# Sums of activations made before the feed-forward loop's first block, and one subtraction for the three low parts of a set

## The chip, the cores and the metric

The kernel runs on one core of one Trainium2 chip. Its time is the device time of one execution in microseconds (us); the time of a version is the median of its runs. The engines are TensorE (PE: matmuls and, overlapped with them, the loads of their stationary operand), VectorE (DVE), ScalarE (ACT), GpSimd (POOL) and SyncE (SP), which issues the large loads.

## The reference

Two attention layers, a feed-forward network (FF1), a mixer layer, a second feed-forward network (FF2) and a gated projection, all in fp32 on 256 tokens of width 2048. The change lies in the feed-forward networks:

```python
def swiglu(x, w_gate, w_up, w_down):
    return (jax.nn.silu(x @ w_gate) * (x @ w_up)) @ w_down
...
    u = rmsnorm_2(h, ff1_pre_g[i])
    h = h + 0.5 * rmsnorm_2(swiglu(u, ff1_w_gate[i], ff1_w_up[i], ff1_w_down[i]), ff1_post_g[i])
```

`w_gate` and `w_up` are 2048 x 5632, `w_down` is 5632 x 2048.

## The kernel before

**Split operands.** Each fp32 operand is held as a high part, a rounded copy made by ScalarE (`w_hi`, `x_hi`), and a low part, the original minus the high part, made by VectorE (`w_lo`, `x_lo`). A product is three matmuls: high by high, high by low, low by high. So VectorE and ScalarE go over every weight that is loaded.

**Blocks.** The hidden width 5632 is worked in `FB` = 11 blocks of 512. Block 0's gate and up products are plain (8 units of weights, `u0` to `u0+7`). Then `first_block_of_hidden` does two things at once: it finishes block 0's hidden values, and makes the gate and up products of the next block; after it come the four down units of block 0 (`down`, `down_added` on VectorE, which adds each 2-bank result to `out2`). Nine further turns (`block_of_hidden`, eight of them in hardware loops or `whole_block(i + 1)`) do the same for the following blocks.

**Seven products instead of eight.** From `first_block_of_hidden` on, gate and up products of a 2 x 2 scheme (two chunks of the contraction, two tiles of tokens) share work through sums: sums of activations (`xs`, made once per network by `x_sums`) and, for each set, three sums of weights (`ff_ws`, made by `first_sum`, `second_sums`, `third_sum`). ScalarE makes the high parts of a set in two instructions (`first_sums_hi` for sums 0 and 1, `third_sum_hi` for sum 2), VectorE the low parts in `sums_lo`. There are 3 sets in `first_block_of_hidden` (p = 1, 2, 3) and 5 in each later block: p = 0 to 3, and a second set for p = 3 (`DOUBLE`), whose activation sums are `half_xs`, made once per network by `half_x_sums` (ten instructions of 128 x 128), with a high part on ScalarE and a low part by `half_x_sums_lo`. TensorE waits for `half_xs_ready` once, just before its loop over the later blocks:

```python
                first_block_of_hidden()
                pe.wait_ge(half_xs_ready, no + 1)
                with pe.Fori(0, FB - 3) as i:
                    block_of_hidden(i + 1)
```

**What sets the order.** Every engine has its own queue, in the order in which this code is written; semaphores tie the queues. The down unit j = 3 uses the PSUM bank that `down_added` of j = 1 reads, so TensorE waits there for VectorE's second addition. SyncE loads a slot of weights when TensorE has used its last content.

Of the kernel before, what the change touches and what calls it, by code (L numbers as in the profile page):

```python
# [7 lines left out]
F32 = mybir.dt.float32  # L8
F32R = mybir.dt.float32r
I32 = mybir.dt.int32  # L10
ACT = mybir.ActivationFunctionType
ALU = mybir.AluOpType
# [70 lines left out]
def build(nc, t):  # L83
# [87 lines left out]
    SUMMED, SUMMED_FIRST, SUMMED_LAST = [0, 1, 2, 3], [1, 2, 3], [0, 1, 2, 3]  # L171
# [31 lines left out]
    with ExitStack() as ctx:  # L203
# [17 lines left out]
        with ExitStack() as masks_space:  # L221
            half_xs_hi = masks_space.enter_context(nc.sbuf_tensor("half_xs_hi", [P, 4, P], F32R))
# [3 lines left out]
        with ExitStack() as masks_space:  # L226
            masks_space.enter_context(nc.sbuf_tensor("ahead_of_half_xs", [P, 4 * P], F32))
            half_xs = masks_space.enter_context(nc.sbuf_tensor("half_xs", [P, 4, P], F32))
# [93 lines left out]
        ff_ws, ff_ws_hi, ff_ws_lo = (ws, other_ws), (ws_hi, other_ws_hi), (ws_lo, other_ws_lo)  # L322
# [1470 lines left out]
        def _(act):  # L1793
# [533 lines left out]
            def feed_forward(b, no, hname):  # L2327
# [4 lines left out]
                def hidden_hi(i, dst=h_hi, bank=6):  # L2332
                    for s in range(2):
                        act.wait_ge(st_turned, i * 2 + (turned_before[hname] + s + 1))
                        nc.scalar.activation(dst[:, 0:UC, s * P:(s + 1) * P],
                                             ps[:, bank + s, :].rearrange("p (k n) -> p k n", k=UC),
                                             ACT.Copy).then_inc(st_hi, 1)
# [33 lines left out]
                def up_second_hi(u, p, i):  # L2371
                    if p == DOUBLE and not (isinstance(i, int) and i == 0):
                        act.wait_ge(ws_made, group(i, p, 1) * 4 + 3)
                    half_hi(u + 2 * p, p, 1, 1, i, plain_hi_ready)
# [44 lines left out]
                def first_block_of_hidden():  # L2419
                    u = u0 + 8  # L2420
                    for p in SUMMED_FIRST:
                        gate_second_hi(u, p, 0)
                        if p == SUMMED_FIRST[0]:
                            x_sums_hi()
                            hidden_hi(0)
                        up_second_hi(u, p, 0)
                        gate_first_hi(u, p, 0)
                        first_sums_hi(0, p)
                        third_sum_hi(0, p)
                        up_first_hi(u, p, 0)  # L2430
                    down_hi(u + 8, 0, 0)
                    first_product_copied(u, 0)
                    down_hi(u + 8, 1, 0)
                    down_hi(u + 8, 2, 0)
# [37 lines left out]
                def whole_block(i):  # L2472
                    if isinstance(i, int):
                        first_block_of_hidden()
                    else:
                        block_of_hidden(i)
                    u = i * 12 + (u0 + 8)
                    down_hi(u + 8, 3, i)
                    hidden_silu(i)
                    next_first_quarter(u + 12, i + 1)  # L2480
                    if isinstance(i, int):
                        act.wait_ge(half_xs_made, 6 * (no + 1))
                        nc.scalar.activation(half_xs_hi[:], half_xs[:], ACT.Copy).then_inc(half_xs_hi_ready, 1)

                whole_block(0)
                with act.Fori(0, FB - 3) as i:
# [153 lines left out]
        def _(dve):  # L2640
# [4 lines left out]
            V = nc.vector  # L2645
# [30 lines left out]
            def splits(u, j0, n):  # L2676
                for k in range(n):
                    split_lo(u + k, (j0 + k) % RAW)
# [737 lines left out]
            def feed_forward(b, no, hname):  # L3416
# [64 lines left out]
                def half_x_sums_lo():  # L3481

                    dve.wait_ge(half_xs_hi_ready, no + 1)
                    V.tensor_tensor(half_xs_lo[:], half_xs[:], half_xs_hi[:].bitcast(F32),  # L3484
                                    ALU.subtract).then_inc(half_xs_ready, 1)
# [22 lines left out]
                def first_sum(u, p, i, h=0):  # L3508

                    n, j = group(i, p, h), 2 * p % RAW  # L3510
                    landed(u + 2 * p, j, h, i)
                    landed(u + (2 * p + 1), j + 1, h, i)
                    since = sums_since(i, p, h)
                    if not isinstance(n, int) or n >= since:
                        dve.wait_ge(ws_used, n - (since - 1))
                    V.tensor_tensor(ff_ws[sums_place(i, p, h)][:, 0], raw_half(p, 1, h)[:, 0], raw_half(p, 0, h)[:, 0],
                                    ALU.subtract).then_inc(ws_made, 1)
# [14 lines left out]
                def sums_lo(p, i, h=0):  # L3532

                    n, place = group(i, p, h), sums_place(i, p, h)
                    dve.wait_ge(ws_made, n * 4 + 4)
                    for m, c in enumerate((slice(0, 2), slice(2, 3))):
                        dve.wait_ge(ws_hi_ready, n * 2 + (m + 1))
                        V.tensor_tensor(ff_ws_lo[place][:, c], ff_ws[place][:, c], ff_ws_hi[place][:, c].bitcast(F32),
                                        ALU.subtract).then_inc(ws_ready, 1)

                def half_lo(p, m, h):

# [22 lines left out]
                def up_second_lo(p, i):  # L3565

                    dve.wait_ge(plain_hi_ready, plain_of(i, p) * 2 + 2)
                    if p == DOUBLE and not (isinstance(i, int) and i == 0):
                        dve.wait_ge(ws_made, group(i, p, 1) * 4 + 3)
                    half_lo(p, 1, 1).then_inc(plain_ready, 1)  # L3570
# [38 lines left out]
                def first_product():  # L3609

                    splits(u0 + 8, 0, 1)
                    x_sums(0)
                    splits(u0 + 9, 1, 1)
                    x_sums(1)
                    dve.wait_ge(ff_silu, h0 + 1)
                    dve.wait_ge(parts_used, u0 + 8)
                    for tt in range(NT):
                        k = V.scalar_tensor_tensor(hid[:, tt], silu[:, tt], rstd[:, tt:tt + 1], ps[:, tt, :],
                                                   ALU.mult, ALU.mult)
                    k.then_inc(hid_ready, 1)  # L3620
                    x_sums(2)
# [5 lines left out]
                    V.tensor_tensor(o, o, ps[:, bank:bank + 2, :], ALU.add).then_inc(added, 1)  # L3627

                splits(u0 + 6, 2, 2)
                first_product()  # L3630
                dve.wait_ge(added, added_before(no))

                def first_block_of_hidden():
                    u = u0 + 8
                    for p in SUMMED_FIRST:
                        gate_second_lo(p, 0)
                        if p == SUMMED_FIRST[0]:
                            x_sums_lo((0,))
                            hidden_lo(0)
                            x_sums_lo((1, 2))  # L3640
                        if p < 3:
                            up_second_lo(p, 0)
                        first_sum(u, p, 0)
                        second_sums(p, 0)
                        third_sum(p, 0)
                        sums_lo(p, 0)
                        gate_first_lo(u, p, 0)
                        up_first_lo(u, p, 0)
                        if p == 3:
                            up_second_lo(p, 0)  # L3650
                    splits(u + 8, 0, 1)
                    first_rest(0)
                    other_rests(0)
                    gates_added(0)
                    splits(u + 9, 1, 1)
                    ups_added(u)
# [44 lines left out]
                def whole_block(i):  # L3701
                    if isinstance(i, int):
                        first_block_of_hidden()
                    else:
                        block_of_hidden(i)
                    u = i * 12 + (u0 + 8)
                    down_added(u + 8, i, 0)
                    splits(u + 10, 2, 2)
                    gate_second_lo(0, i + 1)
                    hidden_product(i)  # L3710
                    if isinstance(i, int):
                        half_x_sums()
                    first_sum(u + 12, 0, i + 1)
                    down_added(u + 8, i, 1)
                    second_sums(0, i + 1)
                    third_sum(0, i + 1)
                    gate_first_lo(u + 12, 0, i + 1)
                    down_added(u + 8, i, 2)
                    sums_lo(0, i + 1)
                    down_added(u + 8, i, 3)  # L3720
                    up_first_lo(u + 12, 0, i + 1)
                    up_second_lo(0, i + 1)
                    if isinstance(i, int):
                        half_x_sums_lo()
                    hidden_lo(i + 1, bank=0)

                whole_block(0)
# [297 lines left out]
```

## Time and profile before

| | |
|---|---|
| median of 3 runs | 2811.15 us (2808.17 to 2815.12) |
| the profiled execution | 2812.0 us |
| its span | 2810.2 us |
| PE busy | 2782.3 us (99%) |
| DVE busy | 2293.3 us (82%) |
| ACT busy | 1499.6 us (53%) |
| FF1's loop and its surroundings, 930 to 1600 us | PE 663.55, DVE 629.01, ACT 361.08 us busy of 670 |
| DMA, mean over the span | 189 GB/s |

A busy time is the union of an engine's instructions; in a row of the timeline the bracket is the time that the engine sat idle before the instruction, with what ended it. Consecutive instructions on one engine overlap at their ends, so a row's duration is a little longer than the distance to the next row. Where the span is longer than PE's busy time, TensorE stood still.

### The profile page before, as it was taken

The numbers are of one execution on the slowest core, as the hardware profiler recorded it, in microseconds if no ns is written. First come the engines' busy times: TensorE is split into PE (matmuls) and PEld (weight loads), VectorE is DVE, ScalarE is ACT, GpSimd is POOL, SyncE is SP. The second block draws the span as 40 slices with busy tenths as digits, with TensorE's granted clock in tenths as the row PEclk, the third lists the DMA queues.
The fourth block names the chain that finished last, engine by engine and source line by source line (L and its number), as shares of the span: only waits on it lengthen the run. The fifth ranks groups of instructions, "written<-read, shape, count | busy, mean of one in ns | idle before, by whom it ended". The sixth has DMA issues, their size and how long they took to land.

```text
span 2810.2 us, 36083 instructions
## 1 busy us (share of the span) xinstructions
PE 2782.3 (99%) x13100; PEld 2322.0 (83%) x13100; DVE 2293.3 (82%) x2684; ACT 1499.6 (53%) x1785; POOL 14.5 (1%) x20
## 2 busy tenths in 40 slices
PE   9999999999999999999999999999999999999998
PEld 8888888888898878888888888888878888888887
DVE  6869857855565889999999877686798999999985
ACT  6544545554545555555555555655554555555564
POOL 0000000000000000000000000000000000000000
PEclk9999999999999999999999999999999999999999
DMA  7546355555545566666666658543566666666654
GB/s 252 199 157 198 117 183 182 194 185 175 165 151 196 179 186 205 200 197 206 201 199 200 206 165 270 179 154 128 195 189 180 199 195 205 198 195 208 214 189 157
DMA packets 279468, 530.74 MB, mean 189 GB/s; under 512 B 12225, under 2 KB 35921, under 8 KB 278849
## 3 DMA queue, kind: packets, MB, share of 16 engines
q1 hardware_dynamic: 278320, 527.02, 59.0%
q0 software_dynamic: 752, 2.04, 0.2%
q8 instruction: 73, 1.20, 0.2%
q14 instruction: 35, 0.28, 0.0%
q10 hardware_dynamic: 288, 0.20, 0.0%
HBM read 527.12 MB, written 2.10 MB: 188 GB/s over the span
## 4 chain that ended last, share of the span: by engine, by line
PE 95%; DVE 3%; DMA 1%; issue 0%; ACT 0%; SPq 0%; DVEq 0%; ACTq 0%
PE ps L867 18%; PE ps L868 18%; PE ps L870 17%; PE ps L1425 9%; PE ps L1427 9%; PE ps L1426 9%; PE ps L878 2%; PE ps L954 1%; PE ps L953 1%; PE ps L952 1%; PE ps L897 1%; PE ps L898 1%; PE ps L902 1%; PE ps L1133 1%; PE ps L1419 1%; PE ps L1113 1%
## 5 line engine op out<-in xcount | busy, mean ns | idle before, releaser
L2664 DVE TENSOR_TENSOR w_lo<-raw,w_hi 128x2048 fp32r<-128x2048 f32 (+4 forms) x301 | 661.2, 2205 | 189.4 <-ACT w_hi L1818 188.3
L1818 ACT ACTIVATE w_hi<-raw 128x2048 fp32r<-128x2048 f32 (+4 forms) x301 | 554.7, 1847 | 287.6 <-DMA raw<-in_ff_w_down 132.9
L867 PE MATMUL ps<-w_hi,x_hi 128*128 128x512 f32 (+4 forms) x1760 | 679.0, 386 | 2.2 <-ACT z L1851 0.9
L868 PE MATMUL ps<-w_lo,x_hi 128*128 128x512 f32 (+4 forms) x1760 | 669.6, 380 | 0.0
L870 PE MATMUL ps<-w_hi,x_lo 128*128 128x512 f32 (+4 forms) x1536 | 582.7, 379 | 0.0
L2359 ACT ACTIVATE w_hi<-raw 128x1024 fp32r<-128x1024 f32 x312 | 321.3, 1049 | 133.0 <-DMA raw<-in_ff_w_up 99.6
L867 PEld LDWEIGHTS ps<-w_hi,x_hi 128*128 128x128 f32 x1760 | 330.7, 188 | 63.5 <-issue 2.5
L868 PEld LDWEIGHTS ps<-w_lo,x_hi 128*128 128x128 f32 x1760 | 330.9, 188 | 58.6
L3544 DVE TENSOR_TENSOR w_lo<-raw,w_hi 128x1024 fp32r<-128x1024 f32 x312 | 373.4, 1218 | 4.5 <-ACT w_hi L2359 2.9
L870 PEld LDWEIGHTS ps<-w_hi,x_lo 128*128 128x128 f32 x1536 | 288.4, 188 | 53.3
L1425 PE MATMUL ps<-w_hi,x_hi 128*128 128x512 f32 x672 | 265.1, 395 | 9.3 <-DVE half_xs_lo L3484 9.2
L1427 PE MATMUL ps<-w_hi,x_lo 128*128 128x512 f32 x672 | 262.8, 391 | 0.0
L1426 PE MATMUL ps<-w_lo,x_hi 128*128 128x512 f32 x672 | 262.7, 391 | 0.0
L867 PE MATMUL ps<-w_hi,h_hi 128*128 128x512 f32 x640 | 250.4, 391 | 3.6 <-DVE z L3627 3.6
L868 PE MATMUL ps<-w_lo,h_hi 128*128 128x512 f32 x640 | 249.7, 390 | 0.0
L870 PE MATMUL ps<-w_hi,h_lo 128*128 128x512 f32 x640 | 249.7, 390 | 0.0
L1425 PEld LDWEIGHTS ps<-w_hi,x_hi 128*128 128x128 f32 x672 | 126.9, 189 | 37.1 <-issue 10.1
L1427 PEld LDWEIGHTS ps<-w_hi,x_lo 128*128 128x128 f32 x672 | 126.8, 189 | 26.7
L1426 PEld LDWEIGHTS ps<-w_lo,x_hi 128*128 128x128 f32 x672 | 127.0, 189 | 25.6
L867 PEld LDWEIGHTS ps<-w_hi,h_hi 128*128 128x128 f32 x640 | 120.5, 188 | 30.4 <-DVE z L3627 4.4
L870 PEld LDWEIGHTS ps<-w_hi,h_lo 128*128 128x128 f32 x640 | 120.5, 188 | 25.3
L868 PEld LDWEIGHTS ps<-w_lo,h_hi 128*128 128x128 f32 x640 | 120.4, 188 | 24.9
(526 smaller groups left out, 3997.3 us busy)
## 6 DMA issues: line engine op xcount, KB each, us to landing
raw<-in_w_in SPq DMA_DIRECT2D x139, 1024.0 KB, 5.1
raw<-in_ff_w_gate SPq DMA_DIRECT2D x144, 512.0 KB, 3.7
raw<-in_ff_w_up SPq DMA_DIRECT2D x144, 512.0 KB, 3.7
raw<-in_ff_w_down SPq DMA_DIRECT2D x144, 512.0 KB, 4.6
raw<-in_w_out SPq DMA_DIRECT2D x45, 1024.0 KB, 5.1
raw<-in_ff_w_gate SPq DMA_DIRECT2D x16, 1024.0 KB, 5.1
raw<-in_ff_w_up SPq DMA_DIRECT2D x16, 1024.0 KB, 5.2
raw<-in_ff_w_down SPq DMA_DIRECT2D x16, 1024.0 KB, 5.2
```

Of the source, the lines that this page charges most:

```text
L867: nc.tensor.matmul(o, x[0][:, k0 + c, s], hi[:, c, 0:width], start=first and c == 0, stop=False)
L868: nc.tensor.matmul(o, x[0][:, k0 + c, s], lo[:, c, 0:width], start=False, stop=False)
L870: m = nc.tensor.matmul(o, x[1][:, k0 + c, s], hi[:, c, 0:width], start=False, stop=last and c == n - 1)
L878: m = nc.tensor.matmul(ps[:, bank + tt, 0:width], x[1][:, k0 + c, tt * P:(tt + 1) * P], hi[:, c, 0:width], start=False, stop=last and c == ...
L897: nc.tensor.matmul(o, x[0][:, k0 + c, s], hi[:, c, 0:width], start=first and c == 0, stop=False)
L1425: nc.tensor.matmul(ps[:, bank, :], x[0], w[0], start=start, stop=False)
L1426: nc.tensor.matmul(ps[:, bank, :], x[0], w[1], start=False, stop=False)
L1427: return nc.tensor.matmul(ps[:, bank, :], x[1], w[0], start=False, stop=stop)
L1818: nc.scalar.activation(landed_part(w_hi, u, j), landed_part(raw, u, j), ACT.Copy).then_inc(hi_ready, 1)
L2359: nc.scalar.activation(w_hi[:, j, c], raw[:, j, c], ACT.Copy).then_inc(ready, 1)
L2664: V.tensor_tensor(landed_part(w_lo, u, j), landed_part(raw, u, j), landed_part(w_hi, u, j).bitcast(F32), ALU.subtract).then_inc(parts_read ...
L3544: return V.tensor_tensor(w_lo[:, j, c], raw[:, j, c], w_hi[:, j, c].bitcast(F32), ALU.subtract)
```

## The change

Three of its edits are one move. `half_x_sums()` goes from the end of block 0's work on VectorE (behind `hidden_product`) to the place behind units `u0+6` and `u0+7`, ahead of `first_product()`. `half_x_sums_lo()` goes from the end of `whole_block(0)` to p = 2 of `first_block_of_hidden`; the ScalarE instruction between the two goes from behind `next_first_quarter` to p = 2 too. The other edit is in `sums_lo`: one subtraction over all three sums, after the second of the two high parts, in the place of one over sums 0 and 1 and one over sum 2.

```diff
@@ ScalarE, first_block_of_hidden
                         if p == SUMMED_FIRST[0]:
                             x_sums_hi()
                             hidden_hi(0)
+                        if p == SUMMED_FIRST[1]:
+                            act.wait_ge(half_xs_made, 6 * (no + 1))
+                            nc.scalar.activation(half_xs_hi[:], half_xs[:], ACT.Copy).then_inc(half_xs_hi_ready, 1)
                         up_second_hi(u, p, 0)
@@ ScalarE, whole_block
                     next_first_quarter(u + 12, i + 1)
-                    if isinstance(i, int):
-                        act.wait_ge(half_xs_made, 6 * (no + 1))
-                        nc.scalar.activation(half_xs_hi[:], half_xs[:], ACT.Copy).then_inc(half_xs_hi_ready, 1)
@@ VectorE, sums_lo
                     dve.wait_ge(ws_made, n * 4 + 4)
-                    for m, c in enumerate((slice(0, 2), slice(2, 3))):
-                        dve.wait_ge(ws_hi_ready, n * 2 + (m + 1))
-                        V.tensor_tensor(ff_ws_lo[place][:, c], ff_ws[place][:, c], ff_ws_hi[place][:, c].bitcast(F32),
-                                        ALU.subtract).then_inc(ws_ready, 1)
+                    dve.wait_ge(ws_hi_ready, n * 2 + 2)
+                    V.tensor_tensor(ff_ws_lo[place][:], ff_ws[place], ff_ws_hi[place][:].bitcast(F32),
+                                    ALU.subtract).then_inc(ws_ready, 2)
@@ VectorE, ahead of the first product
                 splits(u0 + 6, 2, 2)
+                half_x_sums()
                 first_product()
@@ VectorE, first_block_of_hidden
                         if p < 3:
                             up_second_lo(p, 0)
+                        if p == SUMMED_FIRST[1]:
+                            half_x_sums_lo()
                         first_sum(u, p, 0)
@@ VectorE, whole_block
                     hidden_product(i)
-                    if isinstance(i, int):
-                        half_x_sums()
                     first_sum(u + 12, 0, i + 1)
...
                     up_second_lo(0, i + 1)
-                    if isinstance(i, int):
-                        half_x_sums_lo()
                     hidden_lo(i + 1, bank=0)
```

TensorE's queue is the same in both. First place: VectorE at the end of block 0's work in FF1, from `hidden_product` (L3605) on; L3470 to L3479 are `half_x_sums`, L3516 is `first_sum` of the next block's first set, L3627 is `down_added`, L3538 is `sums_lo`, L3544 the low half of a weight unit, L3484 `half_x_sums_lo`. Before:

```order
L3605 SCALAR_TENSOR_TENSOR z<-z,st 128x512 x2
L3470 TENSOR_TENSOR half_xs<-x_hi 128x128
...
L3479 TENSOR_TENSOR half_xs<-half_xs,x_lo 128x128
L3516 TENSOR_TENSOR z<-raw 128x512
L3627 TENSOR_TENSOR z<-z,ps 128x2x512
...
L3538 TENSOR_TENSOR ws_lo<-z,ws_hi 128x1024
L3538 TENSOR_TENSOR ws_lo<-z,ws_hi 128x512
L3627 TENSOR_TENSOR z<-z,ps 128x2x512
L3544 TENSOR_TENSOR w_lo<-raw,w_hi 128x1024 x2
L3484 TENSOR_TENSOR half_xs_lo<-half_xs,half_xs_hi 128x512
L3424 TENSOR_TENSOR h_lo<-ps,h_hi 128x4x128 x2
```

The same place in the changed kernel, where the lines behind `sums_lo` have a number one lower:

```order
L3604 SCALAR_TENSOR_TENSOR z<-z,st 128x512 x2
L3516 TENSOR_TENSOR z<-raw 128x512
L3626 TENSOR_TENSOR z<-z,ps 128x2x512
...
L3537 TENSOR_TENSOR ws_lo<-z,ws_hi 128x1536
L3626 TENSOR_TENSOR z<-z,ps 128x2x512
L3543 TENSOR_TENSOR w_lo<-raw,w_hi 128x1024 x2
L3424 TENSOR_TENSOR h_lo<-ps,h_hi 128x4x128 x2
```

Ten instructions between `hidden_product` and `first_sum` are gone from here, and so is the low part ahead of `h_lo`.

Second place: VectorE of the changed kernel where they went, between the low parts of unit `u0+7` and of `u0+8` (L2664), ahead of `x_sums` (L3439 and on):

```order
L2664 TENSOR_TENSOR w_lo<-raw,w_hi 128x2048 x2
L3470 TENSOR_TENSOR half_xs<-x_hi 128x128
...
L3479 TENSOR_TENSOR half_xs<-half_xs,x_lo 128x128
L2664 TENSOR_TENSOR w_lo<-raw,w_hi 128x2048
L3439 TENSOR_TENSOR xs<-x_hi 128x4x128
```

Before, the same rows read `x3` and then L3439 at once. Third place: VectorE of the changed kernel at p = 1 and p = 2 of `first_block_of_hidden`, with the merged subtraction (L3537) and `half_x_sums_lo` (L3484) behind four halves of weight units:

```order
L3530 TENSOR_TENSOR z<-raw,z 128x512
L3537 TENSOR_TENSOR ws_lo<-z,ws_hi 128x1536
L3543 TENSOR_TENSOR w_lo<-raw,w_hi 128x1024 x4
L3484 TENSOR_TENSOR half_xs_lo<-half_xs,half_xs_hi 128x512
L3516 TENSOR_TENSOR z<-raw 128x512
```

Here the merged instruction stands right behind `third_sum` (L3530), whose high part it now waits for; in the later blocks one or two halves of weight units stand between the two, or the first sums of the next set.

## Rows read from the trace of the kernel before

**Rows 1.** The page: TensorE's and VectorE's busy time.
```profile
PE 2782.3 (99%) x13100; PEld 2322.0 (83%) x13100; DVE 2293.3 (82%) x2684; ACT 1499.6 (53%) x1785; POOL 14.5 (1%) x20
```

**Rows 2.** TensorE's waits: total us, times, longest.
```profile
PE ps L1425 <- DVE half_xs_lo L3484: 9.2, 2, 4.7
PE ps L867 <- DVE z L3627: 3.6, 2, 1.8
```

**Rows 3.** Timeline of TensorE, FF1, block 0's down units and the loop's start.
```profile
1005.27 0.39 PE L867 MATMUL ps<-w_hi,h_hi 128*128 128x512 f32 x1
...
1023.54 0.50 PE L867 MATMUL ps<-w_hi,h_hi 128*128 128x512 f32 x1 [1.79 <-DVE z L3627]
...
1033.93 0.79 PE L1425 MATMUL ps<-w_hi,x_hi 128*128 128x512 f32 x1 [4.66 <-DVE half_xs_lo L3484]
...
1040.43 0.39 PE L1425 MATMUL ps<-ws_hi,xs_first 128*128 128x512 f32 x1
```

**Rows 4.** The same two points of TensorE, and VectorE's `first_sum`, one block later.
```profile
1076.47 0.39 PE L867 MATMUL ps<-w_hi,h_hi 128*128 128x512 f32 x1
...
1090.11 0.68 DVE L3516 TENSOR_TENSOR z<-raw 128x512 f32<-128x512 f32 x1
...
1103.20 0.39 PE L1425 MATMUL ps<-ws_hi,xs_first 128*128 128x512 f32 x1
```

**Rows 5.** The same two points of TensorE in FF2's block 0.
```profile
2079.89 0.39 PE L867 MATMUL ps<-w_hi,h_hi 128*128 128x512 f32 x1
...
2117.71 0.39 PE L1425 MATMUL ps<-ws_hi,xs_first 128*128 128x512 f32 x1
```

**Rows 6.** Stretches: length, each engine's busy time (instructions), granted clock, DMA.
```profile
2096.00:2117.00 21.00, 14.64 (x49) 11.39 (x48) 14.36 (x18) 7.82 (x10) 0.00 (x0) 0.76 0.40 116
...
1020.00:1029.00 9.00, 7.21 (x32) 5.55 (x30) 8.76 (x15) 6.74 (x8) 0.00 (x0) 1.00 0.54 150
```

**Rows 7.** Timeline of VectorE at the end of block 0, FF1.
```profile
1018.91 0.28 DVE L3470 TENSOR_TENSOR half_xs<-x_hi 128x128 f32<-128x128 f32 x1
...
1021.67 0.69 DVE L3516 TENSOR_TENSOR z<-raw 128x512 f32<-128x512 f32 x1
1022.28 1.21 DVE L3627 TENSOR_TENSOR z<-z,ps 128x1024 f32<-128x1024 f32 x1
...
1032.81 0.68 DVE L3484 TENSOR_TENSOR half_xs_lo<-half_xs,half_xs_hi 128x512 fp32r<-128x512 f32 x1
```

**Rows 8.** Groups of VectorE from 951.8 to 961.5 (FF1), 2026.8 to 2036.2 (FF2).
```profile
L2664 DVE TENSOR_TENSOR w_lo<-raw,w_hi 128x2048 fp32r<-128x2048 f32 x2 | 4.6, 2292 | 2.9 <-ACT w_hi L1818 2.9
L2664 DVE TENSOR_TENSOR w_lo<-raw,w_hi 128x2048 fp32r<-128x2048 f32 x2 | 4.6, 2292 | 2.6 <-ACT w_hi L1818 2.6
```

**Rows 9.** Timeline at p = 2 and p = 3 of block 0, FF1: ScalarE, VectorE.
```profile
979.93 1.06 ACT L2359 ACTIVATE w_hi<-raw 128x1024 fp32r<-128x1024 f32 x1 [1.56 <-DMA raw<-in_ff_w_up]
989.90 1.22 DVE L3544 TENSOR_TENSOR w_lo<-raw,w_hi 128x1024 fp32r<-128x1024 f32 x1 [0.70 <-ACT w_hi L2359]
992.65 0.69 DVE L3516 TENSOR_TENSOR z<-raw 128x512 f32<-128x512 f32 x1 [1.52 <-PE ps L1427]
```

**Rows 10.** Timeline of the third set, FF1: ScalarE, VectorE, TensorE's weight load.
```profile
995.30 0.63 ACT L2389 ACTIVATE ws_hi<-z 128x512 fp32r<-128x512 f32 x1
995.44 1.83 DVE L3538 TENSOR_TENSOR ws_lo<-z,ws_hi 128x1024 fp32r<-128x1024 f32 x2 [0.17 <-ACT ws_hi L2384]
997.56 0.19 PEld L1425 LDWEIGHTS ps<-ws_hi,xs_fourth 128*128 128x128 f32 x1
```

**Rows 11.** VectorE's groups by form, whole span: count, busy us, mean ns.
```profile
L3538 DVE TENSOR_TENSOR ws_lo<-z,ws_hi 128x1024 fp32r<-128x1024 f32 x60 | 73.1, 1218 | 0.5 <-ACT ws_hi L2384 0.3
L3538 DVE TENSOR_TENSOR ws_lo<-z,ws_hi 128x512 fp32r<-128x512 f32 x60 | 41.0, 683 | 0.0
```

**Rows 12.** The loop's tightest set: VectorE's subtractions, TensorE's weight load.
```profile
2393.61 1.82 DVE L3538 TENSOR_TENSOR other_ws_lo<-z,other_ws_hi 128x1024 fp32r<-128x1024 f32 x2
2395.82 0.19 PEld L1425 LDWEIGHTS ps<-other_ws_hi,xs_fourth 128*128 128x128 f32 x1
```

## Prediction

> **What bounds the kernel now.** I read the busy shares first. TensorE is busy 2782.3 us of a span of 2810.2 [rows 1], so it bounds the kernel and 27.9 us of standstill are all that an edit of other engines can win directly. TensorE's waits come next: who kept it? Two lines stand out, and both belong to the two feed-forward networks, once in each: 9.2 us for `half_xs_lo` and 3.6 us for `down_added` (L3627), together 12.8 us of the 27.9 [rows 2]. No wait for `ws_lo` or for any low part inside the loop is among them: the eighteen later blocks run without a gap on TensorE. So the change can gain only at block 0 of FF1 and FF2, and whatever it saves in the loop on VectorE is slack.
>
> Then the timeline at that place. After the long wait, TensorE does not take up its pace: in FF1 the first matmul takes 0.79 us where the ones further on take 0.39 [rows 3]. In FF2 the granted clock is 0.76 over the 21 us from the first wait on, so nearly half of them ran at 1.2 GHz instead of 2.4 [rows 6]. So a wait costs more than its length. I therefore don't add up waits, but measure the whole detour between two fixed points of TensorE's program: the first down matmul of block 0 and the first matmul on sums of weights of the next block. In FF1 that takes 1040.43 - 1005.27 = 35.16 us [rows 3]; one block later, with the same instructions and no wait, 1103.20 - 1076.47 = 26.73 us [rows 4]. The detour is 8.43 us. In FF2 it is 2117.71 - 2079.89 - 26.73 = 11.09 us [rows 5]. Together 19.52 us: 12.8 of waits and 6.7 of slow clock.
>
> **The move, what it removes.** Behind `hidden_product` ten small instructions take 1021.67 - 1018.91 = 2.76 us of VectorE [rows 7]. The second `down_added` stands behind them: it started at 1022.28 and will start at 1019.52, to end 1.21 us later at 1020.73. TensorE wants it when it has done three down units: its wait of 1.79 us ended at 1023.54, so it was done at 1021.75, less 0.16 for the overlap of two matmuls at the end, 1021.6 [rows 3]. 0.86 us to spare, so this wait goes altogether. The second wait is for `half_xs_ready`, whose low part ended at 1032.81 + 0.68 = 1033.49 [rows 7]; it is now made some 50 us earlier. What is late next there? With both gone TensorE comes to the loop at 1005.27 + 4 x 5.44 = 1027.0 (a down unit takes a third of 1021.6 - 1005.27). What it needs then are the third `down_added` and the low half of a weight unit. VectorE's remaining queue, shifted by 2.76 us or to the end of the TensorE unit that it adds, is then what it is in the later blocks: there L3516 starts 1090.11 - 1076.47 = 13.64 us behind the first down matmul [rows 4], here it will be 1018.91 - 1005.27 = 13.64 too, and those blocks have no wait. I take the whole detour, 19.52 us, as gained. From both sides: at least the 12.8 us of waits if the clock should drop anyway, at most 19.52.
>
> **The move, what it adds.** Nothing is added, three pieces stand elsewhere. The ten instructions (2.76 us) go ahead of unit `u0+8`'s low part. VectorE stood idle there, before that one and the next unit, for 2.9 us in FF1 and 2.6 in FF2, each time for ScalarE and the loads behind it [rows 8]. The 2.76 fill that; 0.2 us may stick out in FF2, with more idle time behind. Without this cover it would be 2.76 us of VectorE, some 15 us ahead of TensorE's need. The ScalarE piece (0.61 us) goes ahead of the instruction at 979.93, which waited 1.56 us for a load anyway [rows 9]. The low part (0.68 us, 0.61 to the next instruction) goes to p = 2; what it delays there is counted with the next edit. SyncE's and GpSimd's queues are not passed: cost 0.
>
> **One subtraction instead of two.** The form 128x1536 is not in the trace. 128x1024 takes 1218 ns, 128x512 takes 683, so 512 elements cost 535 ns and 128x1536 should take 1.75 us [rows 11]; half way from 1218 to the 2292 ns of 128x2048 [rows 8] is 1.76. It saves about 0.08 us of VectorE's queue in each of the 96 sets (the two took 1.83 together [rows 10]), 8 us in all, and none of it where TensorE waits: worth 0. What it costs is that sums 0 and 1 are ready later. In the loop the high part of sum 2 is done before VectorE comes to the subtraction, since other work stands between, so the delay is 1.75 - 1.22 = 0.53 us. The tightest of the 90 sets there: start 2393.61, end 2395.36 where the first ended at 2394.83; TensorE's first weight load comes at 2395.82 [rows 12]. 0.46 us to spare: cost 0.
>
> In block 0 the merged one stands right behind `third_sum` and has to wait for ScalarE's 0.63 us. Sets 1 and 2 push VectorE back by 0.6 us each, and the moved low part by 0.6 more: 1.8 us, before p = 3, against idle times of 0.70 and 1.52 us on the way [rows 9]. Absorbed. Set 3 is left: ScalarE's high part ends at 995.93, the merged one runs from about 996.0 to 997.75, and TensorE's weight load that needs it came at 997.56 [rows 10]. With a handover of 0.05 us (VectorE's L3627 ended at 1023.49 and TensorE started at 1023.54 [rows 3, 7]) TensorE stands for 0.25 us. Bounds: 0, if the handovers are shorter, and 0.5, if each takes longer. Twice, so 0.5 us lost.
>
> **The sum.** 19.5 gained, 0.5 lost: 19.0 us off the profiled execution's own 2812.0, which is 2793.0 us. That execution was 0.85 us above the median of the runs shown, 2811.15. Since the slow clock behind the waits differs from network to network (2.0 us in FF1, 4.7 in FF2) it will differ from run to run as well, and with it goes part of the 7 us spread of before. The time after has none of it, so I keep 2793 and take nothing off for the median. A change of under 0.3% (8.4 us) is about what a measurement of this kernel can't tell from none.
>
> **Rivals.** *Part of it stays.* If `first_sum` of the next block must wait for its load (in later blocks such waits occur), the second `down_added` comes later, and past 0.86 us TensorE waits again; or the loop's first block, entered 8 us sooner, has one short wait for a load. Against it: the same order works without a wait in the later blocks. Price: up to the 3.6 us of L3627 and up to one slow stretch of clock in each network (2.0 us by FF1): 2793 + 3.6 + 4.0 = 2800.6, middle 2798. Chance 0.13.
>
> *Short waits bring the slow clock.* The new wait of 0.25 us is small, but it could cost more than itself. For it: the waits for L3627 were 1.8 us long in both networks, and after FF2's the stretch shows 0.76; against it: after FF1's, of equal length, the granted clock is 1.00 [rows 6], and the new one is a seventh as long. Price 2 x 2.0 to 2 x 4.7 us: 2797 to 2802. Chance 0.05. The Trainium skill has such a rule ("TensorE: Matmul & The Clock Gate", section "A second HAM failure mode: psum-queue depth-cycling"): short idle times between groups of matmuls, if there are many, make the clock swing between its levels. By that rule the merged subtraction would be dear; that FF1's wait of 1.79 us left the clock at 1.00 speaks against it here.
>
> *Nothing moves.* The waits return elsewhere, because VectorE or the loads, not their order, limit block 0: TensorE would wait in the loop's first block for what it now reaches late. For it: VectorE is busy 8.76 of the 9 us from 1020 on [rows 6]. Against it: later blocks hold the pace of 26.73 us with the same work [rows 4]. Time within 0.3%, 2803 to 2811. Chance 0.06.
>
> *Slower.* The merged subtraction makes TensorE wait in the loop: one place, p = 3, five sets a block, 18 blocks. It has 0.46 us to spare at its tightest [rows 12]. To end 8.4 us above before it must cost 19.5 + 8.4 = 28 us, 1.5 us a block, so the sums would have to be ready 2 us later than worked out, with 1.75 us an instruction of more than 3.5. No row is near that: 2820. Chance 0.02.
>
> **How the numbers follow.** The forecast, 2793, has 0.74, with its own range from 2789 (no new wait, a somewhat faster execution) to 2797. The first two rivals reach to 2802. I put the range at 2788 to 2801.5; outside it are the last two rivals, 0.08, and some 0.08 of the others. Faster by over 0.3% (below 2802.7) are the forecast and the first two rivals, less a little for the unforeseen: 0.90. Same 0.07, slower 0.03.
>
> **What would show it.** Right: no row of TensorE waiting for `half_xs_lo` or for `down_added`; between the two fixed points 26.7 us in both networks; granted clock 1.00 from block 0's down units on; a wait of 0.2 to 0.3 us for `ws_lo` ahead of `xs_fourth`, once in each; VectorE's busy time 6 to 14 us lower; the form 128x1536 at 1.75 us. Wrong: a wait of TensorE for `ws_lo` inside the loop, or for a load in its first block; a slow clock behind the short wait in block 0.

## The result, and the profile after

The changed kernel takes 2792.03 us (median of 4 runs, 2791.79 to 2792.41), the kernel before beside it 2811.97 us (4 runs, 2808.17 to 2815.12): a ratio of 0.993, interval 0.9913 to 0.9947. The forecast was 2793.0 us. Its profiled execution took 2791.79 us, 20.2 less than that of before. The four runs scatter over 0.6 us where those of before scattered over 7. Of the runs told below, two of one kernel (3473 and 10009 us) stand far outside all others, for a reason that no trace shows, and are left out.

The page's first rows, the span and the busy times, beside [rows 1]:

```profile
span 2790.0 us, 35987 instructions
...
PE 2775.6 (99%) x13100; PEld 2318.9 (83%) x13100; DVE 2286.9 (82%) x2588; ACT 1499.7 (54%) x1785; POOL 14.5 (1%) x20
```

TensorE does the same 13100 matmuls in 6.7 us less busy time: that is not work saved, but clock. While TensorE works, the trace of before has it at half in four places, this one in one, in the mixer. VectorE has 96 instructions fewer and is busy 6.4 us less. TensorE's waits, the longest first, beside [rows 2]:

```profile
PE ps L897 <- ACT x_hi L2023: 1.7, 1, 1.7
PE ps L1304 <- POOL ones L818: 1.0, 1, 1.0
PE ps L867 <- ACT z L1851: 0.8, 1, 0.8
```

Both lines of [rows 2] are gone; what leads now lies outside the feed-forward networks. The two fixed points of TensorE, in FF1 and then in FF2, beside [rows 3] and [rows 5]:

```profile
1005.36 0.39 PE L867 MATMUL ps<-w_hi,h_hi 128*128 128x512 f32 x1
...
1027.12 0.39 PE L1425 MATMUL ps<-w_hi,x_hi 128*128 128x512 f32 x1
...
1032.12 0.39 PE L1425 MATMUL ps<-ws_hi,xs_first 128*128 128x512 f32 x1
...
2071.75 0.39 PE L867 MATMUL ps<-w_hi,h_hi 128*128 128x512 f32 x1
...
2098.52 0.39 PE L1425 MATMUL ps<-ws_hi,xs_first 128*128 128x512 f32 x1
```

26.76 and 26.77 us, where [rows 4] had 26.73: block 0 now runs like a later block. TensorE comes to the loop at 1027.12. The same stretches by engine (length; busy us of PE, PEld, DVE, ACT, POOL; granted clock; DMA), beside [rows 6]:

```profile
1005.00:1033.00 28.00, 28.00 (x129) 23.25 (x128) 26.77 (x26) 14.71 (x15) 0.00 (x0) 1.00 0.73 218
2071.00:2099.00 28.00, 28.00 (x130) 23.23 (x129) 26.78 (x25) 14.71 (x15) 0.00 (x0) 1.00 0.74 224
```

The clock is 1.00 in both. The one new cost is at the third set of block 0, beside [rows 10]: ScalarE's high part of sum 2, VectorE's merged subtraction, TensorE's weight load and matmul.

```profile
995.16 0.62 ACT L2389 ACTIVATE ws_hi<-z 128x512 fp32r<-128x512 f32 x1
...
995.91 1.76 DVE L3537 TENSOR_TENSOR ws_lo<-z,ws_hi 128x1536 fp32r<-128x1536 f32 x1 [0.90 <-ACT ws_hi L2389]
...
997.72 0.19 PEld L1425 LDWEIGHTS ps<-ws_hi,xs_fourth 128*128 128x128 f32 x1 [0.45 <-DVE ws_lo L3537]
...
997.30 0.39 PE L1427 MATMUL ps<-w_hi,x_lo 128*128 128x512 f32 x1
997.72 0.50 PE L1425 MATMUL ps<-ws_hi,xs_fourth 128*128 128x512 f32 x1
998.05 0.40 PE L1426 MATMUL ps<-ws_lo,xs_fourth 128*128 128x512 f32 x1
```

VectorE stood 0.90 us for the high part. The matmuls start 0.42 and 0.33 us apart in the place of 0.227 each, so TensorE lost 0.30 us. In FF2 they start 0.32 and 0.33 us apart, 0.20 us lost. The list of waits has neither: they fell into the overlap of two matmuls' ends, and show in the distances and in the weight load's bracket. The weight load in FF2:

```profile
2064.12 0.19 PEld L1425 LDWEIGHTS ps<-ws_hi,xs_fourth 128*128 128x128 f32 x1 [0.35 <-DVE ws_lo L3537]
```

The merged form and the moved sums, from VectorE's groups and timeline, beside [rows 11] and [rows 8]:

```profile
L3537 DVE TENSOR_TENSOR ws_lo<-z,ws_hi 128x1536 fp32r<-128x1536 f32 x60 | 105.2, 1754 | 4.9 <-ACT ws_hi L2389 4.9
...
951.40 0.29 DVE L3470 TENSOR_TENSOR half_xs<-x_hi 128x128 f32<-128x128 f32 x1
...
954.16 2.29 DVE L2664 TENSOR_TENSOR w_lo<-raw,w_hi 128x2048 fp32r<-128x2048 f32 x1
...
959.03 2.29 DVE L2664 TENSOR_TENSOR w_lo<-raw,w_hi 128x2048 fp32r<-128x2048 f32 x1
```

The ten instructions take 2.76 us again, and the low part of the unit behind them follows without idle time.

### The profile page after: what moved, and what is told of

It is laid out like the page before. It is cut to its first block, busy times and chain, and to the rows that moved or that the text cites. A ratio compares the mean times of both kernels' runs of the same rounds, so it can differ in the third digit from the quotient of the medians.

```text
span 2790.0 us, 35987 instructions
## 1 busy us (share of the span) xinstructions
PE 2775.6 (99%) x13100; PEld 2318.9 (83%) x13100; DVE 2286.9 (82%) x2588; ACT 1499.7 (54%) x1785; POOL 14.5 (1%) x20
## 4 chain that ended last, share of the span: by engine, by line
PE 98%; DVE 1%; DMA 0%; ACT 0%; issue 0%; SPq 0%; DVEq 0%; ACTq 0%
PE ps L867 19%; PE ps L868 19%; PE ps L870 17%; PE ps L1425 9%; PE ps L1427 9%; PE ps L1426 9%; PE ps L878 2%; PE ps L954 1%; PE ps L953 1%; PE ps L952 1%; PE ps L897 1%; PE ps L898 1%; PE ps L902 1%; PE ps L1133 1%; PE ps L1419 1%; PE ps L1113 1%
## 5 line engine op out<-in xcount | busy, mean ns | idle before, releaser
L2664 DVE TENSOR_TENSOR w_lo<-raw,w_hi 128x2048 fp32r<-128x2048 f32 (+4 forms) x301 | 661.5, 2207 | 183.9 <-ACT w_hi L1818 183.0
```

What stands on the lines that cost most here:

```text
L2664: V.tensor_tensor(landed_part(w_lo, u, j), landed_part(raw, u, j), landed_part(w_hi, u, j).bitcast(F32), ALU.subtract).then_inc(parts_read ...
```

## The experiments

All were timed beside the kernel before, four kernels to a chip. The edits are to the changed kernel unless said otherwise.

**The move alone.** `sums_lo` as before the change (two subtractions).

> The sums of activations are moved as in the change, the low parts of a set stay two instructions. Theory (the order at block 0's end is what the change gains, the merged subtraction costs its wait ahead of the third set): 0.6 us under the changed kernel's 2792.0, so 2791.4, no short wait at the third set (0.30 us in each network there), the stretch between the two fixed points 26.7 us. Rival 1 (the merged subtraction gives part of the gain, since VectorE is slower by 0.08 us a set without it): above 2793. Rival 2 (the two effects need each other): above 2797, with a wait for down_added back.

Measured: 2790.55 us (5 runs, 2790.05 to 2792.22), ratio 0.9926 (0.9914 to 0.9939). It has the whole gain. The changed kernel on the same chip had 2790.72, so the merged subtraction gives no part of it, and the 0.6 us that the moved sums alone were expected to be ahead can't be told in the medians (0.2 us apart); the spans of the profiled executions are 2788.8 and 2788.9 us. In its trace the matmuls at the third set start 0.23 us apart: the short wait is gone.

**The merged subtraction alone**, in the kernel before:

```diff
-                    for m, c in enumerate((slice(0, 2), slice(2, 3))):
-                        dve.wait_ge(ws_hi_ready, n * 2 + (m + 1))
...
+                    dve.wait_ge(ws_hi_ready, n * 2 + 2)
+                    V.tensor_tensor(ff_ws_lo[place][:], ff_ws[place], ff_ws_hi[place][:].bitcast(F32),
+                                    ALU.subtract).then_inc(ws_ready, 2)
```

> The kernel before with the merged subtraction alone. Theory: no gain, both waits stay (3.6 us for down_added, about 9.1 for half_xs_lo), one short wait of 0.3 us more in each network: within 2 us of the kernel before, so 2810 to 2814. VectorE's busy time about 6.5 us lower all the same. Rival (the merge gives part of the 20 us): 2808 or less.

Measured: 2811.5 us (11 runs, 2809.90 to 2813.61), the kernel before 2811.45 (17 runs); ratio 1.0 (0.9991 to 1.0009). Its page's busy times and its TensorE's waits:

```profile
PE 2780.7 (99%) x13100; PEld 2321.3 (83%) x13100; DVE 2287.2 (81%) x2588; ACT 1500.1 (53%) x1785; POOL 14.5 (1%) x20
...
PE ps L1425 <- DVE half_xs_lo L3484: 9.2, 2, 4.6
PE ps L867 <- DVE z L3626: 3.6, 2, 1.8
```

VectorE is busy 6.1 us less than in [rows 1], the two waits are the same to a tenth, and so is the time: nearly all of the work was saved where nobody waits for VectorE.

**Two subtractions in block 0, one in the later blocks**, run on two chips.

```diff
+                    if isinstance(i, int) and i == 0:
+                        for m, c in enumerate((slice(0, 2), slice(2, 3))):
...
+                        return
```

> The changed kernel with two instructions for the low parts in the three sets of block 0 and one in the later blocks. Theory: the 0.3 us wait ahead of the third set goes in both networks, 2791.4, the same as the move alone, as what the merged one saves in the loop is slack. Rival (the saving in the loop counts, because TensorE is kept now and then for a few tenths by VectorE there): 0.5 us or more under the move alone, 2790.9 or less.

> The changed kernel with two instructions for the low parts in block 0 and one in the later blocks, once more beside the changed kernel. Theory: 0.5 to 0.7 us under it by the trace (the two short waits ahead of the third sets), which is less than the runs scatter.

Measured: 2791.94 us over the four other runs of the first chip (2790.40 to 2792.94), and 2791.24 (5 runs, 2790.38 to 2792.57) on the second, where the changed kernel had 2791.54. The short wait is gone from the trace: TensorE's matmuls at the third set, first of this kernel on the second chip, then of the changed kernel there:

```profile
997.32 0.39 PE L1427 MATMUL ps<-w_hi,x_lo 128*128 128x512 f32 x1
997.54 0.39 PE L1425 MATMUL ps<-ws_hi,xs_fourth 128*128 128x512 f32 x1
```

```profile
997.71 0.39 PE L1427 MATMUL ps<-w_hi,x_lo 128*128 128x512 f32 x1
998.36 0.50 PE L1425 MATMUL ps<-ws_hi,xs_fourth 128*128 128x512 f32 x1 [0.27 <-DVE ws_lo L3537]
```

Here the changed kernel lost 0.53 us at this set in FF1, more than the 0.30 of its first profile. Spans: 2788.3 against 2788.9 us on the first chip, 2788.2 against 2789.8 on the second. Its profiled executions are the shortest of all, but that it is the best version isn't shown: beside the changed kernel its median is 1.2 us above on the first chip and 0.3 us below on the second, and the runs scatter by 2 us. The rival, 2790.9 or less, did not come; the saving in the loop is not told from nothing.

**The changed kernel again**, as the measure for the tenths of the others.

> The changed kernel once more, on the chip of the three others, so that tenths of a microsecond can be compared: 2792.0, within 0.5 us.

> The changed kernel on the chip of the three others: 2790.5 to 2792.5.

Measured: 2790.72 us (2790.33 to 2791.85), missed by more than the 0.5 allowed, and 2791.54 (2791.34 to 2792.49), as expected. Between the profiled executions the span differs by 1.1 us (2790.0 and 2788.9), and 0.9 of it lies between the mixer and FF2's first down matmul. In the mixer TensorE waits 1.7 us for `x_hi` (L897) in each of them. The stretch around that wait, first in the changed kernel's first profile, then in its second (2790.72 us):

```profile
1615.00:1630.00 15.00, 13.00 (x60) 10.27 (x59) 12.98 (x19) 7.65 (x13) 0.00 (x0) 0.89 0.35 113
```

```profile
1615.00:1630.00 15.00, 12.73 (x67) 10.14 (x67) 14.13 (x21) 7.95 (x14) 0.00 (x0) 1.00 0.38 119
```

The same wait is followed by slow clock once and once not: seven matmuls more in the same 15 us. It isn't all that differs between executions: the third profile of this kernel has clock 1.00 there and a span of 2789.8 us, as it came to FF1's first down matmul 0.7 us later than the second (1005.97 against 1005.28).

**The ten instructions one place later**, in the kernel before: behind the second `down_added` in the place of ahead of it.

```diff
-                    if isinstance(i, int):
-                        half_x_sums()
                     first_sum(u + 12, 0, i + 1)
                     down_added(u + 8, i, 1)
+                    if isinstance(i, int):
+                        half_x_sums()
```

> The kernel before with the ten small instructions put behind the second down_added instead of ahead of it, the rest as before. Theory (VectorE's chain from block 0's end to the low part of the half sums is what TensorE waits for, and its length stays the same): the wait for down_added goes, 3.6 us in the two networks, and the wait for half_xs_lo grows by the same, to about 6.4 us each. Time as before, 2810 to 2813. Rival (each of the two waits is a cost of its own): 3.6 us faster, 2807.

Measured: 2809.44 us (10 runs, 2807.73 to 2811.09) against 2810.57 (15 runs), ratio 0.9996 (0.9987 to 1.0005). The one row of its waits that lies in the feed-forward networks:

```profile
PE ps L1425 <- DVE half_xs_lo L3484: 13.5, 2, 6.7
```

The wait for `down_added` is gone and came back in the other one: 13.5 us where there were 9.2 + 3.6 = 12.8. The two waits hang on one chain of VectorE's work, which has no idle time from the last weight unit to the low part and takes 19.24 us in FF1 with either order (from 1014.25 to 1033.49 before, from 1014.00 to 1033.25 here). Counted apart, this edit would have been worth 3.6 us. The time is a little under the 2810 to 2813 expected, and its interval just reaches the rival's 3.6 us; it is the list of waits that decides.

**The low part late.** Sums and high part early, `half_x_sums_lo()` taken out at p = 2 and put at the end of VectorE's block 0:

```diff
                     up_second_lo(0, i + 1)
+                    if isinstance(i, int):
+                        half_x_sums_lo()
                     hidden_lo(i + 1, bank=0)
```

> The changed kernel with the ten small instructions and the high part early, but the low part of the half sums back at the end of VectorE's work of block 0. Theory (two waits, each with its own producer; the ten instructions were behind the first, the place of the low part behind the second): no wait for down_added, but VectorE's low part ends at about 1031.4 in FF1 where TensorE arrives at 1027.1, so a wait of about 4.7 us with 0.4 us of loop entry in each network, and slow clock of 2 to 3.5 us behind it: 2790.7 + 9.4 + 5.5 = 2805.5. Rival (it is VectorE's total work at block 0's end that counts, and 2.76 us less of it frees both waits): 2792 to 2796.

Measured: 2805.49 us (10 runs, 2803.42 to 2806.63), ratio 0.9982 (0.9972 to 0.9991). TensorE's wait, the stretches around it in FF1 and FF2, and VectorE's fourth `down_added` in FF1:

```profile
PE ps L1425 <- DVE half_xs_lo L3484: 9.2, 2, 4.6
...
1027.00:1042.00 15.00, 10.43 (x39) 8.35 (x38) 9.35 (x11) 4.56 (x6) 0.00 (x0) 0.77 0.37 105
2101.00:2116.00 15.00, 10.41 (x44) 8.34 (x43) 9.80 (x13) 5.08 (x7) 0.00 (x0) 0.89 0.41 122
...
1028.77 1.22 DVE L3626 TENSOR_TENSOR z<-z,ps 128x1024 f32<-128x1024 f32 x1 [0.57 <-PE ps L870]
```

One instruction of 0.6 us in the wrong place costs about 14 us in two networks: it stands behind the fourth `down_added`, which here itself waits for TensorE, and two low halves of 1.1 us each. So with the ten instructions away the first wait goes and the second stays as long as it was: VectorE's chain got shorter by 2.8 us, but spends 0.57 of them waiting, and TensorE comes 1.8 us earlier.

**The low part right behind, and right ahead of, the fourth `down_added`.** The diff is the one ahead; the other has the call one line lower. In both it is taken out at p = 2.

```diff
                     sums_lo(0, i + 1)
+                    if isinstance(i, int):
+                        half_x_sums_lo()
                     down_added(u + 8, i, 3)
```

> The same with the low part right behind the fourth down_added. Theory: it ends at about 1029.1 in FF1, a wait of 2.4 us in each network. What comes on top is slow clock, somewhere from 0 to 3.5 us a network: 2795.6 without it, up to 2802 with it in both. Rival (the wait alone is the cost, no clock effect): 2795.6 with a granted clock of 1.00 behind it.

> The same with the low part right ahead of the fourth down_added, in VectorE's idle time there. Theory: it ends at about 1027.4 in FF1, 0.3 us after TensorE arrives; with the loop entry a wait of 0.3 to 0.7 us in each network and no slow clock: 2791.3 to 2792.1. Rival (a short wait brings the slow clock): 2794 or more.

Measured behind: 2796.69 us (4 runs, 2796.25 to 2799.20). The wait and the clock:

```profile
PE ps L1425 <- DVE half_xs_lo L3484: 4.6, 2, 2.3
...
1024.00:1039.00 15.00, 12.70 (x60) 10.27 (x59) 13.43 (x15) 8.34 (x10) 0.00 (x0) 1.00 0.56 167
2092.00:2107.00 15.00, 12.71 (x61) 10.27 (x60) 13.45 (x16) 8.25 (x10) 0.00 (x0) 1.00 0.58 172
```

Two waits of 2.3 us and no slow clock: of the 2795.6 to 2802 expected, the end without it. Measured ahead: 2794.9 us (4 runs, 2793.60 to 2795.85), more than the 2792.1 allowed and over the rival's 2794. But the rival's reason isn't there, the clock behind the waits is 1.00 in both networks. Its waits, and the mixer's stretch:

```profile
PE ps L1425 <- DVE half_xs_lo L3484: 1.5, 2, 0.9
...
1617.00:1632.00 15.00, 13.29 (x62) 10.56 (x61) 13.00 (x20) 6.81 (x14) 0.00 (x0) 0.89 0.38 119
```

The waits are 0.61 and 0.87 us, and from the first down matmul to the loop TensorE lost 0.77 and 1.03 us against the changed kernel, together 1.8 where 0.6 to 1.4 were allowed. The slow clock in the mixer is part of the surplus over 2790.7, but the changed kernel's first profile has it too, and this span is 2.3 us longer than that one (2792.3 and 2790.0): 1.8 of them are the two waits, 0.5 stay open. So does the median, 0.8 us above the profiled execution.

**Additions that nobody reads**, behind `hidden_product`, five or two of them:

```diff
                     hidden_product(i)
+                    if isinstance(i, int):
+                        for _ in range(5):
+                            link(V.tensor_tensor(half_xs_low[:], x_lo[:, 14, 0:P].bitcast(F32),
+                                                 x_lo[:, 15, 0:P].bitcast(F32), ALU.add))
```

> The changed kernel with five linked additions of 128x128 that nobody reads, between hidden_product and first_sum at block 0's end: 1.6 us of VectorE at the place of the ten. Theory (0.87 us to spare for the second down_added): a wait of 0.75 us in each network, 2790.7 + 1.5 = 2792.2. Rival (VectorE has no time to spare there, or everything behind is late as well): 1.6 us or more a network, 2794 or more.

> The changed kernel with two linked additions that nobody reads at block 0's end, 0.65 us of VectorE. Theory: within the 0.87 us to spare of the second down_added, no wait of TensorE, the time of the changed kernel, 0 to 0.2 us more. Rival (the five additions of the run before cost 0.9 us a network because all of VectorE's time there counts in part): 0.35 us a network, 0.7 us more, and a row of TensorE waiting for down_added.

Measured with five: 2793.84 us (4 runs, 2792.86 to 2794.92), which is 1.6 us over the 2792.2 expected and near the rival's 2794. The profiled execution, the fastest of the four, took 2792.86, its span is 2790.7. Its wait for `down_added`:

```profile
PE ps L867 <- DVE z L3626: 1.3, 2, 0.7
```

Between the first down matmul and the loop TensorE takes 22.72 us in each network where the changed kernel takes 21.76: 0.96 us lost in each, more than the 0.75 expected and less than the rival's 1.6. Why the other three runs are slower than the profiled one isn't known.

With two: 2791.53 us (5 runs, 2790.82 to 2794.07), the changed kernel beside it 2791.54, and no such row. VectorE's second `down_added` and TensorE's first matmul that needs it:

```profile
1020.21 1.21 DVE L3626 TENSOR_TENSOR z<-z,ps 128x1024 f32<-128x1024 f32 x1
...
1021.63 0.40 PE L867 MATMUL ps<-w_hi,h_hi 128*128 128x512 f32 x1
```

It ended at 1021.42, with 0.65 us of surplus work ahead of it, 0.2 us before TensorE came. With the 1.6 us of the five, TensorE's matmul starts at 1022.48, 0.81 us later than here, counted from the first down matmul. Both put the time to spare at 0.8 us, near the 0.86 of the forecast.

## Why the prediction was right

**What bounds it.** Right: TensorE, and only at block 0. The merged subtraction alone saved 6.1 us of VectorE's work and 0 of time.

**The detour as the unit of the gain.** 19.52 us were forecast; measured between the fixed points 35.16 - 26.76 = 8.40 in FF1 and 37.82 - 26.77 = 11.05 in FF2, 19.45. Had I added the waits alone I would have been 6.7 us short. That the slow clock is part of the cost is shown: the low part late brings the long wait back without the short one, and with it clocks of 0.77 and 0.89. The size of the slow part in one trace is a matter of chance, though: with the merged subtraction alone and the same waits, the detours are 9.9 and 9.8 us, where the trace of before had 8.4 and 11.1; with the ten instructions one place later they are 8.8 and 8.5, 2.1 less in all, with 0.7 us more of waits. So the agreement of 19.45 with 19.52 shows that all of the detour went; that the time came out within 1 us of the forecast is in part luck.

**The step least well put** is that the two waits are removed one by one, each by its own part of the move, and nothing is said of the chain that they share. The ten instructions one place later show it: for the whole move the sum comes out the same, but removing the first wait alone gains nothing that can be told from none.

**What is late next: nothing.** Right. TensorE came to the loop at 1027.12, forecast 1027.0. The second `down_added` had 0.8 us to spare, as the two and the five additions show.

**The covers.** The ten instructions behind unit `u0+7` took up idle time: the unit behind them started 0.2 us later than before in FF1 (954.16 against 953.96), the next one at 959.03, 0.4 us earlier than before. In FF2 more stuck out than the 0.2 us forecast: measured from the unit ahead, the unit behind them was 0.9 us late, the next one 0.1. The low part at p = 2 and the waits of sets 1 and 2 (0.80 us each, forecast 0.6) were absorbed before p = 3, where VectorE's `first_sum` started at 992.39, before at 992.65.

**The merged subtraction.** 128x1536 takes 1754 ns, forecast 1.75 us. The wait at the third set cost 0.30 us in FF1, where 0.25 stood, since VectorE started 0.13 us after ScalarE's end and not 0.05, and 0.20 in FF2: the 0.5 of the forecast. Other executions of the same kernel had 0.2 to 0.5 us. No wait for `ws_lo` in the loop is on the list.

**Short waits and the clock.** This rival fell for the change itself: behind the new waits of 0.3 us, and behind those of 0.6 to 0.9 and of 2.3 us in the experiments, the clock was 1.00. The prediction's argument against it was too strong, though: it had the clock at 1.00 behind FF1's 1.79 us and left open what the 0.76 in FF2 came from. A narrower view of the trace of before shows that the clock fell there right behind the wait of 1.80 us for `down_added`, which ended at 2098.16 (length; TensorE's busy us and matmuls; granted clock; DMA):

```profile
2098.00:2100.00 2.00, 1.84 (x5) 0.62 0.66 240
2100.00:2102.00 2.00, 2.00 (x7) 0.53 0.00 0
2102.00:2106.00 4.00, 3.50 (x16) 1.00 0.44 127
```

The rule of the Trainium skill that the prediction weighed ("TensorE: Matmul & The Clock Gate", section "A second HAM failure mode: psum-queue depth-cycling") is one of frequent short idle times, and the merged subtraction brings two in a run; no run here has them frequent, so none tests it.

**The scatter.** The prediction gave the time after no slow clock at all. It has none at block 0, but the changed kernel's first profile has some in the mixer; the kernel before has it there too, so it drops out of the 20.2 us.

**The rest.** The profiled executions differ by 20.2 us, 1.3 more than 19.45 - 0.50. 1.0 of it lies behind FF2's block 0 (2810.2 - 2117.71 = 692.5 against 2790.0 - 2098.52 = 691.5). It belongs to that one execution and not to the change: the two other profiles with the old order, the merged subtraction alone and the ten instructions one place later, have 691.4 and 691.5 us there. What it was is open; medians of the same kernel on different chips (2792.03, 2790.72, 2791.54) differ by as much.

## What to carry to other kernels

Measure what a wait costs between two fixed points of the waiting engine's program and compare with an undisturbed pass over the same instructions; the list of waits gives a lower bound, as it knows neither the slow clock nor the restart. When two waits follow each other on one engine, ask whether they have one chain of work behind them: then only what takes work away from ahead of the last awaited piece counts, by moving the work or the piece, and not the order of what stays ahead of it. Work that depends on nothing recent, done once in a queue just where its consumer arrives, belongs into an idle time long before, and merging instructions is worth nothing where the merged engine has slack, and costs what its last input is late where it has none.

## What the runs showed of the hardware

What the granted clock does behind a standstill of TensorE isn't settled by the length of the standstill alone. Behind waits of 4.6 us and more it was at half in each network of each trace that had them (eight cases). Behind 2.3 us (two cases) it stayed at 2.4 GHz. Behind the 1.8 us of `down_added` it fell in one case of four: in FF2 of the kernel before, by the rows shown above, but not in FF1 there, nor in either network with the merged subtraction alone. The mixer's wait of 1.71 us is in all 14 profiles; behind it the clock fell in four (the kernel before, the changed kernel's first profile, the ten instructions one place later, the low part right ahead) and stayed at 1.00 in ten. From the mixer's matmuls just ahead of that wait (L1057) to FF2's first down matmul the four took 455.8 to 456.3 us, the ten 454.6 to 455.6. That is most of the 1.1 us of span between the two executions of the same kernel; how much of the scatter of the runs without a profile comes from it isn't shown.

A wait also costs more than its length at a clock of 1.00. With the five additions the list has a wait of 0.66 us, and each network lost 0.96 us. Part of the difference is the overlap of two matmuls' ends, about 0.16 us, which the list doesn't count. The rest is the restart: the matmul behind the wait took 0.50 us in the place of 0.39, and the next one started 0.34 us behind it in the place of 0.23.
